# Branch output products of a transformer trunk as three products of rounded pieces, with split weights in two small buffers

## What is computed

```python
mix = (jax.nn.sigmoid(g_att) * jnp.einsum('bsc,cd->bsd', att, lw['w_att_o'])
       + jax.nn.sigmoid(g_ret) * jnp.einsum('bsc,cd->bsd', ret, lw['w_ret_o'])
       + jax.nn.sigmoid(g_mlp) * jnp.einsum('bsc,cd->bsd', cm, lw['w_mlp_o']))
x = x + gate1 * jnp.einsum('bsd,de->bse', mix, lw['w_out'])
```

## Time and profile before

| what | value |
|---|---|
| median of 3 runs | 2362.5 us (2361.3 to 2365.04) |
| the profiled execution's own time | 2362.1 us |
| its span, first to last instruction | 2360.2 us |
| mean granted TensorE clock | 0.946 |
| PE busy | 2148.0 us (91%), 10495 matmul records |
| PE weight loads busy | 1604.8 us (68%) |
| DVE (VectorE) busy | 1234.7 us (52%) |
| ACT (ScalarE) busy | 802.6 us (34%) |
| POOL (GpSimd) busy | 261.9 us (11%) |

### The profile page before, as it was taken

How to read it: one execution, slowest core, us unless ns; L and a number is a source line. 1 busy time by engine, 2 the same in 40 slices (tenths; PEclk the granted TensorE clock), 3 DMA queues, 4 the chain that set the end, 5 groups by cost and what they waited for, 6 DMA issues and landing times.

```text
span 2360.2 us, 25654 instructions
## 1 busy us (share of the span) xinstructions
PE 2148.0 (91%) x10495; PEld 1604.8 (68%) x10495; DVE 1234.7 (52%) x1632; ACT 802.6 (34%) x1018; POOL 261.9 (11%) x212
## 2 busy tenths in 40 slices
PE   4999999999999969999659999999999996799991
PEld 1686555588886548888537765647888845688881
DVE  1495335222222369888456743442222234788883
ACT  2214522100000137778432254111000011578871
POOL 2142010200000020100111401101000000100102
PEclk7999999999999969999879999999999996899996
DMA  9124620311214279999532244021212133699984
GB/s 366 43 109 161 248 47 1 125 36 72 103 41 170 107 274 404 411 414 403 215 148 71 112 177 144 10 72 54 97 47 72 68 120 143 253 415 410 415 340 152
DMA packets 95095, 417.08 MB, mean 177 GB/s; under 512 B 7496, under 2 KB 9592, under 8 KB 64128
## 3 DMA queue, kind: packets, MB, share of 16 engines
q1 hardware_dynamic: 70656, 329.27, 36.1%
q0 software_dynamic: 19536, 68.25, 7.6%
q10 hardware_dynamic: 4784, 17.87, 1.9%
HBM read 378.85 MB, written 36.50 MB: 176 GB/s over the span
## 4 chain that ended last, share of the span: by engine, by line
PE 89%; DVE 5%; DMA 3%; ACT 1%; issue 1%; PEldq 0%; POOL 0%; ACTq 0%; DVEq 0%; POOLq 0%
PE ps L660 77%; PE ps L784 3%; PE ps L796 2%; PE ps L672 2%; DMA ring_lo<-in_w_in_dram 1%; PE ps L1086 1%; PE ps L857 1%; PE ps L1097 1%; DMA work<-y_dram,slots_u 1%; PE ps L785 1%; DVE work L1969 1%; DVE work L1971 1%; DVE work L1972 1%; DMA const<-in_persistent_dram 0%; DMA work<-h_dram,slots_u 0%
## 5 line engine op out<-in xcount | busy, mean ns | idle before, releaser
L1926 DVE TENSOR_TENSOR expert_low<-ring_lo,expert_high 128x2048 fp32r<-128x2048 f32 x172 | 386.3, 2286 | 2.1 <-ACT expert_high L1449 2.0
L1449 ACT ACTIVATE expert_high<-ring_lo 128x2048 fp32r<-128x2048 f32 x172 | 326.3, 1914 | 104.9 <-PE ps L660 88.2
L660 PE MATMUL ps<-ring_lo,hT 128*128 128x512 f32 (+1 forms) x800 | 324.4, 562 | 22.7 <-ACT hT L1253 12.4
L660 PEld LDWEIGHTS ps<-ring_lo,hT 128*128 128x128 f32 x800 | 152.9, 195 | 172.9 <-issue 168.0
L660 PE MATMUL ps<-expert_high,x_high 128*128 128x512 f32 x512 | 207.3, 405 | 9.6 <-DVE expert_low L1926 9.6
L660 PE MATMUL ps<-branch,ring_lo 128*128 128x320 f32 x768 | 214.4, 432 | 0.0
L660 PE MATMUL ps<-expert_high,x_low 128*128 128x512 f32 x512 | 201.9, 394 | 0.0
L660 PE MATMUL ps<-expert_low,x_high 128*128 128x512 f32 x512 | 200.7, 392 | 0.0
L1398 ACT ACTIVATE work<-ps 128x640 f32<-128x640 f32 x48 | 33.8, 704 | 485.5 <-PE ps L660 485.4
L660 PE MATMUL ps<-h_hi,w_hi 128*128 128x320 f32 x768 | 186.2, 324 | 2.6 <-issue 2.6
L660 PEld LDWEIGHTS ps<-branch,ring_lo 128*128 128x128 f32 x768 | 143.5, 190 | 53.3
(11 more groups left out here) (277 smaller groups left out, 3267.1 us busy)
## 6 DMA issues: line engine op xcount, KB each, us to landing
ring_lo<-in_w_up_dram SPq DMA_DIRECT2D x64, 1024.0 KB, 8.1
ring_lo<-in_w_gate_dram SPq DMA_DIRECT2D x54, 1024.0 KB, 7.9
ring_lo<-in_w_down_dram SPq DMA_DIRECT2D x54, 1024.0 KB, 8.3
ring_lo<-in_w_in_dram SPq DMA_DIRECT2D x26, 2048.0 KB, 7.9
ring_lo<-in_w_mod_dram SPq DMA_DIRECT2D x24, 2048.0 KB, 11.5
y_dram<-branch ACTq DMA_DIRECT2D x32, 512.0 KB, 8.3
work<-in_w_down_dram SPq DMA_DIRECT2D x10, 1024.0 KB, 8.2
work<-in_w_gate_dram SPq DMA_DIRECT2D x10, 1024.0 KB, 8.8
```

What stands on the lines that cost most here:

```text
L660: return pe.matmul(out, lhsT, rhs, start=(k == 0), stop=(k == n - 1))
L1449: A(e_high[n % HIGH], e_raw[n % RAW], ACT.Copy).then_inc(ec_a.sem, 1)
L1926: TT(out=e_low[n % RAW], in0=e_raw[n % RAW], in1=e_high[n % HIGH].bitcast(F32), op=ALU.subtract).then_inc(el_v.sem, 1)
```

## The change

The branch product is made as the gate product is, from three products of rounded pieces. VectorE splits a branch's values into branch_high and branch_low (branch_high and branch_low in the code are the two steps; the low part is written in place, over branch), and the output weights of a turn, 4 x 128 columns, into one of two buffers o_high and a low part in the slot (split_o). The high parts of branches 0 and 2 and o_high0 lie over constants in small (retention tables and gains) that are no longer read in the layer; that of branch 1 and o_high1 lie in work, where mix_tmp and gate1 were. So the temporary mix_tmp goes (the product is written over the sigmoid), gate1 moves by 128 columns, and its loads on GpSimd wait for branch product 16 instead of the gating.

```diff
+        at_small = after_h + 12 * T + -(-PERSISTENT.shape[1] // 8) * 8
+        b_high = [rounded(f"branch{b}_high", at_small if b % 2 == 0 else 4 * SLOT + 14592, 4 * T) for b in range(3)]
+        b_low = [rounded(f"branch{b}_low", after_h + 4 * T * b, 4 * T) for b in range(3)]
+        o_high = [rounded("o_high0", at_small + 4 * T, 512), rounded("o_high1", 4 * SLOT + 17152, 512)]
...
-        mix_tmp = w_(14592, 640)
-        gate1 = w_(15232, 2 * D).rearrange("p (s d) -> p s d", s=2)
+        gate1 = w_(15104, 2 * D).rearrange("p (s d) -> p s d", s=2)
...
-                        for half in range(2):
-                            for k in range(4):
-                                i = mm(bank(4 + b + half, T // 2), wo[:, k * D + c * P:k * D + (c + 1) * P],
-                                       src[:, k, half * T // 2:(half + 1) * T // 2], k, 4)
+                        w(pe, bs_v, l, br + 1)
+                        w(pe, os_v, l, n + 1)
+                        for k in range(4):
+                            wo = o_high[n % 2][:, k * P:(k + 1) * P]
+                            products = ((wo, src_high), (wo, src_low),
+                                        (o_low[:, k * D + c * P:k * D + (c + 1) * P], src_high))
+                            for m, (wk, sk) in enumerate(products):
+                                for half in range(2):
+                                    i = mm(bank(4 + b + half, T // 2), wk, sk[:, k, half * T // 2:(half + 1) * T // 2],
+                                           3 * k + m, 12)
                         i.then_inc(o3_p.sem, 1)
...
+                def branch_high(br):
+
+                    step.do(V.tensor_copy(b_high[br], branch[:, 4 * T * br:4 * T * (br + 1)]))
+
+                def branch_low(br):
+
+                    TT(out=b_low[br], in0=branch[:, 4 * T * br:4 * T * (br + 1)], in1=b_high[br].bitcast(F32),
+                       op=ALU.subtract).then_inc(bs_v.sem, 1)
+
+                def split_o(n):
+
+                    br, c = divmod(n, KD)
+                    key = (l, f"o{br}")
+                    V.wait_ge(full[slot_of[key]], full_at(key))
+                    raw, rest = (m[slot_of[key]].rearrange("p (k c) -> p k c", k=4)[:, :, c * P:(c + 1) * P]
+                                 for m in (slot, slot_r))
+                    high = o_high[n % 2].rearrange("p (k c) -> p k c", k=4)
+                    step.do(V.tensor_copy(high, raw))
+                    TT(out=rest, in0=raw, in1=high.bitcast(F32), op=ALU.subtract).then_inc(os_v.sem, 1)
+
...
+                w(V, vn_v, l, NT)
+                w(V, at_a, l, NT * HQ // 2)
+                branch_high(0)
+                branch_low(0)
                 w(V, st_out, l, 32)
...
+                split_o(0)
+                split_o(1)
 
                 for n in range(24):
...
-                        step.do(TT(out=in_halves(mix_tmp), in0=in_halves(sg[n % 2]), in1=prod, op=ALU.mult))
-                        TT(out=mixT[:, c, :], in0=mixT[:, c, :], in1=mix_tmp, op=ALU.add).then_inc(mix_v.sem, 1)
+                        step.do(TT(out=in_halves(sg[n % 2]), in0=in_halves(sg[n % 2]), in1=prod, op=ALU.mult))
+                        TT(out=mixT[:, c, :], in0=mixT[:, c, :], in1=sg[n % 2], op=ALU.add).then_inc(mix_v.sem, 1)
+                    if n + 2 < 24:
+                        split_o(n + 2)
                     if n + 3 < 24:
                         split_gate(n + 3)
+                    if n == 2:
+                        w(V, cm_p, l, NT)
+                        w(V, rt_ev, l, NT)
+                        branch_high(1)
+                    if n == 3:
+                        branch_low(1)
+                    if n == 8:
+                        w(V, cm_a, l, NT)
+                        branch_high(2)
+                    if n == 9:
+                        branch_low(2)
...
-                w(G, cm_v, l, NT)
+                w(G, o3_p, l, 16)
```

More of the change, by code:

```diff
@@ L344, in trunk @@
         wg_v = signal("gate_split", 24)
+        bs_v = signal("branch_split", 3)
+        os_v = signal("o_split", 24)
         g_p = signal("gate_product", 24)
@@ L975, in _ @@
                 lo3 = h_lo.rearrange("p (k t) -> p k t", k=KD)
-                for br, src in enumerate((attT, retT, cmT)):
-                    wo = None
+                for br in range(3):
+                    o_low = slot_r[slot_of[l, f"o{br}"]]
+                    src_high, src_low = (m[br].rearrange("p (k t) -> p k t", k=4) for m in (b_high, b_low))
                     for c in range(KD):
                         n = 8 * br + c
-                        if c == 0:
-                            wo = loaded(f"o{br}")
                         b = 2 * (n % 2)
```

## The result

The changed kernel takes 2324.14 us (median of 4 runs, 2322.27 to 2326.67) where the kernel before takes 2361.9 (4 runs): a ratio of 0.9841, 95% interval 0.9829 to 0.9852. The forecast was 2324.5. Timed again later, the same kernel took 2322.3 us (5 runs), ratio 0.983 (0.9817 to 0.9843).

What follows compares the result with a forecast made beforehand. TensorE, matmuls busy for 91% of the span, was taken to bound the kernel. Branch products save 38.0 us over 48 turns, all else priced at nothing: from the 2362.5 median, 2324.5 us, range 2319 to 2331.

Steps and rivals of the forecast that it cites:

- The branch block: TensorE's branch products in each turn: eight fp32 products, 4.31 us, become 24 rounded passes, 3.52 us; 48 turns give 38.0 us.
- The two bounds: Price of a branch pass: 0.142 us at the experts' rate (gain 43.7 us), or 0.188 us with the weight load bare.
- the Trainium skill's isolated gap: Pass priced at its columns over 2.4 GHz and 2.5 ns: 136 ns for 320 columns, gain 50 us, time 2312.
- The weight load as a rival: Branch block's 24 passes: loads not hidden cost 188 ns a pass, block 4.51 us, time 2372 us; chance 3%.
- The splits on VectorE: Casts and subtractions for weights and branches: 79 us more of VectorE, covered by TensorE's turn and priced at nothing.
- Before the loop: Splits ahead of the gate block, the first branch's 4.34 us included: covered, at most 1 us a layer.
- the worse of its two cases: First branch's subtraction stands behind all 2.34 us of GpSimd's: gating ends at 431.3, 1.6 us of cover left.
- Waits and queues: TensorE's two new waits, GpSimd's later gate1 loads and SyncE's slot loads: all met in time, nothing added.
- After the loop: Load of x before the fourth output product: 0.8 us slack shrinks by 0.79; nothing or a tenth, up to 1 us a layer.

Runs made afterwards that it cites:

- the longer prologue: Changed kernel plus three 128x1024 VectorE reductions behind the split of the first branch, ahead of the first spatial gating: 2324.78 us, ratio 0.9837.

## Why the prediction was right

*The branch block: right.* 4.31 us to 3.51, a turn from 11.34 to 10.55, forecast 3.52 and 10.55. The rate that was taken from the gate block held for the branch block to a hundredth of a microsecond, and taking away 8 of its passes a turn gave back just their 0.1465 us each. The two bounds, 0.142 and 0.188 us a pass, were not reached. That the median came within 0.4 us of the forecast is partly luck: the runs of the kernel scatter from 2322.27 to 2326.67 us, and the second series gave 2322.3. Nor is the Trainium skill's isolated gap (TensorE: Matmul & The Clock Gate, Back-to-back issue gap) the price here; 136 ns was an estimate by it, 0.1465 us is measured in every kernel of this study with passes of 320 columns.

*The weight load as a rival: wrong in this kernel, but its mechanism exists.* It said that a pass of 320 columns costs its load of 188 ns. It costs 147, and the load lies under the neighbouring passes. Behind a pass of 128 columns the load does hold TensorE: in the kernel with 512 and 128 columns the loads are never closer than 0.108 us, and 0.05 to 0.06 us a pair are lost one pass later. No run has passes of 128 columns alone in a branch block, so the price of a row of them is not measured. The load's own record (188 ns in the mean) is a bad price for it: the records of two loads overlap.

*The splits on VectorE: right.* 79 us more were forecast, and its busy time went from 1234.7 to 1314.4 us. None shows: with fp32 products and the splits kept the stage is as before, and 3.5 us more a turn on top are still free.

*Before the loop: right, by the worse of its two cases.* The subtraction of the first branch stood behind GpSimd. The timeline of VectorE and GpSimd:

```profile
424.59 1.49 DVE L1754 CAST branch_high<-branch 128x2560 fp32r<-128x2560 f32 x1
426.12 4.86 DVE L1758 TENSOR_TENSOR branch_low<-branch,branch_high 128x2560 fp32r<-128x2560 f32 x1
430.90 1.11 DVE L1790 SCALAR_TENSOR_TENSOR work<-ps,small,work 128x128 f32<-128x128 f32 x4
```

```profile
425.77 2.53 POOL L2145 TENSOR_TENSOR h_lo<-hT,h_hi 128x1024 fp32r<-128x1024 f32 x1 [81.22 <-PE ps L665]
```

The subtraction takes 4.86 us, where 2.82 is usual; of GpSimd's instruction 2.18 us are left when it starts (426.12 to 428.30), and the subtraction is 2.04 longer. The gating ends at 432.0, TensorE turns its result at 434.10, so 2.1 us of cover are left where 1.6 were forecast, and the longer prologue measured the same 2.1. By the Trainium skill (SBUF — State Buffer, SBUF: two separate sides) an instruction of VectorE that reads two operands from SBUF and one of GpSimd that reads SBUF exclude each other, and the one that comes second is held until the other is done. The row agrees, with 2.04 us of the 2.18.

*Waits and queues: right.* The gate1 loads behind branch product 16 alone gave 0.9999.

*After the loop: right within what was allowed.* The cover of x's transfer was to shrink from 0.8 us to none. In this profile the transfer is quicker: VectorE starts on it 21.6 us after its issue, where it was 22.7.

```profile
712.71 0.87 POOL L2157 DMA_DIRECT2D hT<-x_dram  x1
...
734.31 0.69 DVE L1836 TENSOR_TENSOR work<-ps,work 128x512 f32<-128x512 f32 x1 [5.21 <-DMA hT<-x_dram]
735.04 0.69 DVE L1837 TENSOR_TENSOR hT<-hT,work 128x512 f32<-128x512 f32 x1
```

The bank is free at 735.73 and the fourth product starts at 716.18 + 20.7 = 736.9: 1.1 us of slack, all of it from the quicker transfer: by the forecast's 22.7 us there would be none. So this is the next thing to bind in the first layer.

## What to carry to other kernels

An fp32 matmul here costs 0.54 us for 320 columns, three rounded passes 0.44: splitting saves a fifth of TensorE's time, if another engine has the room for the splits, and the price of a pass is best taken from start to start of neighbouring passes of the same shape, not from busy time, which pointed the wrong way. The longer the pass, the better it pays (512 columns: 0.86 us against 3 x 0.227 = 0.68); pieces of 128 columns would turn it round by an estimate. A plain fp32 product of 128 columns takes 0.22 us in the change's trace (the four spatial gating products, eight records, start from 425.45 us, and the next product starts at 426.34). Three rounded passes, whose loads are 0.108 us apart at the least, would be at 0.32 us or more. The output products and the gMLP's are still plain fp32 in this kernel and the next candidates; that was not tried here.

## What had not been expected

- A pair of 512 and 128 columns costs 0.345 us where 384 and 256, or 320 and 320, cost 0.293. The 128-column pass is followed by the next after 0.06 us, and the loss shows one pass later, at the load.
- The weight-load row was full, 242.00 of 242.00 us, in a stage of rounded passes at 320 columns, and at 215 with part of it in fp32, while the matmul row read full in both. A full row of loads did not mean that loads set the pace: 12 passes of 512 columns and 23 pairs of 320 differ by their columns (0.2267 and 0.1465 us a pass, 0.080 for 192 columns).
- Two series gave 0.9976 (0.9966 to 0.9985) and 0.9993 (0.9984 to 1.0002) for one kernel. An interval from one series can be narrower than what differs between series; a difference of a quarter of a per cent wants a control and a second series.
- The records of VectorE's instructions overlap by some 0.08 us where one does not wait for the other: six reductions of 1.21 us in 6.84 us. Where one needs the other's result they don't: in the turn above, the cast at 600.12 ends at 600.54 and its subtraction starts at 600.57. Summing durations overstated VectorE's chain by most of 14 us a layer here.
